# Parameter loads spread over three issuing queues in the opening of a two-layer hybrid SSD, Hyena and mLSTM kernel

## What is computed

```
mod  = silu(c) @ w_mod[i] + b_mod[i]          # six vectors of 1024, for latent and context
u    = modulated_norm(x, norm1_w[i], mod[0], mod[1]) @ w_in[i]
z, xbc, dt, hy_u, qk, v, o, g = split(u)      # three mixers: SSD, Hyena, mLSTM
hyena: uc = short_conv(hy_u, hy_conv_w, hy_conv_b)
       filt = (sin-MLP(feats) @ hy_pos_w3) * exp(-t * |hy_decay|), normalised, transformed
       z = gate * (long_conv(z, filt) + hy_skip * z), twice
x    = x + mod[2] * (concat(mixers) @ w_out[i])
x    = x + mod[5] * hier_moe(modulated_norm(x, norm2_w[i], mod[3], mod[4]))   # 32 experts, top-2
```

## Time and profile before

| | |
|---|---|
| median of 3 runs | 1327.77 us (1325.08 to 1328.37) |
| the profiled execution | 1324.55 us |
| its span in the profile | 1322.6 us |
| PE busy | 1170.5 us, 88% of the span |
| DVE busy | 605.8 us, 46% |
| ACT busy | 305.9 us, 23% |
| POOL busy | 133.2 us, 10% |
| DMA | 323.50 MB, mean 245 GB/s |

### The profile page before, as it was taken

The page is one execution under the profiler, slowest core; times in us unless marked ns, Lnnn a source line. Parts: engine busy times, 40 slices in busy tenths (PEclk is TensorE's granted clock), DMA queues, the critical chain, the costliest instruction groups (busy, mean ns, idle before and its releaser), DMA issues. The chain is left out here.

```text
span 1322.6 us, 19488 instructions
## 1 busy us (share of the span) xinstructions
PE 1170.5 (88%) x7596; PEld 769.2 (58%) x7596; DVE 605.8 (46%) x1233; ACT 305.9 (23%) x623; POOL 133.2 (10%) x144
## 2 busy tenths in 40 slices
PE   6799999999899979999877689998889899988882
PEld 3444547987678855555444466467768655545551
DVE  4424996037973641343111266973393533332223
ACT  4201112254552202131111233141442100000001
POOL 0000000000000012222221100000000112221220
PEclk9799999998999979999898899998999899998997
DMA  8653233236663579999999755441484879999982
GB/s 289 194 163 98 94 111 96 86 123 198 205 243 101 234 249 384 391 388 376 374 385 387 268 188 166 127 139 49 159 273 189 345 306 388 386 389 390 403 340 113
DMA packets 146965, 323.50 MB, mean 245 GB/s; under 512 B 28249, under 2 KB 111254, under 8 KB 121912
## 3 DMA queue, kind: packets, MB, share of 16 engines
q1 hardware_dynamic: 135384, 306.17, 63.8%
q0 software_dynamic: 11392, 15.79, 3.7%
q10 hardware_dynamic: 96, 0.26, 0.0%
HBM read 321.37 MB, written 22.28 MB: 260 GB/s over the span
## 5 line engine op out<-in xcount | busy, mean ns | idle before, releaser
L657 PE MATMUL bank<-hT,ring 128*128 128x512 f32 (+1 forms) x544 | 207.9, 540 | 1.8 <-DVE hT L1784 1.8
L657 PE MATMUL bank<-ring,hT 128*128 128x256 f32 (+1 forms) x928 | 180.3, 349 | 8.7 <-DVE chain L1794 3.9
L657 PEld LDWEIGHTS bank<-ring,hT 128*128 128x128 f32 x928 | 154.3, 194 | 27.8 <-issue 7.2
L657 PEld LDWEIGHTS bank<-hT,ring 128*128 128x128 f32 x544 | 104.5, 194 | 98.9 <-issue 91.9
L1788 DVE TENSOR_TENSOR ktok<-ktok,bank 64x256 f32<-64x256 f32 x65 | 27.5, 423 | 278.2 <-ACT ktok L1401 198.0
L657 PE MATMUL bank<-chain,qkT 128*64 128x256 f32 (+1 forms) x760 | 138.8, 380 | 6.1 <-DMA chain<-in_moe_w_up 2.7
L1401 ACT ACTIVATE ktok<-bank 64x256 f32<-64x256 f32 (+2 forms) x79 | 32.1, 406 | 346.9 <-PE bank L657 295.0
L657 PE MATMUL bank<-ring,qkT 128*64 128x256 f32 x512 | 92.7, 409 | 15.8 <-DMA ring<-in_moe_w_up 7.7
L1334 POOL DMA_INDIRECT pair_rows<-hyT,ysum x65 | 65.7, 1011 | 382.5 <-ACT hyT L1401 194.9
L657 PEld LDWEIGHTS bank<-chain,qkT 128*64 128x64 f32 (+1 forms) x760 | 82.6, 150 | 26.1 <-issue 4.8
L657 PEld LDWEIGHTS bank<-ring,qkT 128*64 128x64 f32 x512 | 56.3, 147 | 33.4 <-issue 15.1
(11 more groups left out here) (298 smaller groups left out, 1748.1 us busy)
## 6 DMA issues: line engine op xcount, KB each, us to landing
ring<-in_w_mod SPq DMA_DIRECT2D x40, 1024.0 KB
ring<-in_w_in SPq DMA_DIRECT2D x22, 1024.0 KB
chain<-in_moe_w_up SPq DMA_DIRECT2D x21, 1024.0 KB
chain<-in_moe_w_gate SPq DMA_DIRECT2D x19, 1024.0 KB
ring<-in_moe_w_down SPq DMA_DIRECT2D x18, 1024.0 KB
chain<-in_moe_w_down SPq DMA_DIRECT2D x17, 1024.0 KB
ring<-in_moe_w_gate SPq DMA_DIRECT2D x16, 1024.0 KB
ring<-in_moe_w_up SPq DMA_DIRECT2D x16, 1024.0 KB
```

The source lines that it names most:

```text
L657: return nc.tensor.matmul(o, a, b, start=s, stop=e, **k)
```

## The change

The small loads of the opening leave SP. ACT issues the six of the filter network, and POOL the rest, in the order: `tcol`, taps, the modulation biases of layer 0, norm weights, `dft`, the 9 rows of `prow`; then it waits until modulation part 7 is made and issues the gate columns and weights, the modulation biases of layer 1, the constants and the router's parameters (37 DMAs). `prow` has a semaphore of its own. SP issues the identity, the conditioning vectors, the tokens and then only large weights. The instructions of PE, ACT and DVE in the opening stand in another order, and the first `hy` block waits for `hT` column by column instead of for all of it, in both layers.

```
@@ small loads by a function that takes the engine, prow on its own semaphore
+        def fetch(eng, group, dst, src):
+            with nc.allow_non_contiguous_dma(reason="small parameters"):
+                eng.dma_start(dst, src).then_inc(tally.sems[group], tick(group, (group,), by=16))
...
+                fetch(eng, f"prow{l}_in", prow[r:r + n, :], src)
@@ SP, opening
-                    hidden_parameters(0)
-                    tap_parameters(0)
+                    fetch(sp, "cond_in", ident[:, :], A["const_ident"])
+                    fetch(sp, "cond_in", cond_v[:, :, 0], A["c"][0].rearrange("(p k) -> p k", k=KB))
+                    fetch(sp, "cond_in", cond_v[:, :, 1], A["c_ctx"].rearrange("(p k) -> p k", k=KB))
+                    fetch(sp, "x_in", x_v[:, 0:2, :], A["ctx"][0].rearrange("(t p) d -> p t d", p=P))
...
                     first_pair(0)
...
-                    fetch("dft_in", dft[:, :], A["const_dft"])
                     first_single(6)
-                    for layer in range(DEPTH):
-                        fetch("mod_bias_in", bmod_v[:, layer], A["b_mod"][layer].rearrange("(m p k) -> p m k", m=6, k=KB))
-                    norm_weights(0)
                     first_single(7)
@@ PE
                     filter_step(l, 2)
-                    modulation(l, 0)
-                    modulation(l, 1)
+                    pe.wait_ge(*due(("cond",)))
+                    for n in range(6):
+                        modulation(l, n)
+                    mod_vector(l, 0)
                     filter_step(l, 3)
...
-                    filter_step(l, 4)
-                    filter_step(l, 5)
                     modulation(l, 6)
                     modulation(l, 7)
                     mod_vector(l, 1)
...
-                    small_columns()
-                    pe.wait_ge(*due(("h1T", l, 0)))
-                    pe.wait_ge(*due(("h1T", l, 1)))
...
-                    pe.wait_ge(*due(("h1T", l, 1, "act")))
-                    pe.wait_ge(*due(("h1T", l, 1, "dve")))
...
+                            if (name, blk) == ("hy", 0):
+                                for s in range(1 if a0 else 0, 2):
+                                    pe.wait_ge(*due(("h1T", l, s, k)))
                             last = mm(b[:, a0:512], w[:, k, i * P:(i + 1) * P], hT_v[:, k, a0:512],
...
+                        if (l, name, blk) == (0, "hy", 0):
+                            small_columns()
...
                     channel_major("hy", 6, q, lambda blk: n0)
+                    if l == 0 and q == 0:
+                        pe.wait_ge(*due(("four",)))
+                        filter_step(l, 4)
+                        filter_step(l, 5)
@@ POOL, ahead of everything else
+            fetch(pool, "taps0_in", tcol[:, :], A["const_tcol"])
+            tap_parameters(pool, 0)
...
+            mod_biases(0)
+            norm_weights(pool, 0)
+            fetch(pool, "dft_in", dft[:, :], A["const_dft"])
+            parameters(pool, 0)
+            pool.wait_ge(*due(("made", ("mod", 0, 7))))
+            gate_parameters(pool, 0)
+            mod_biases(1)
+            for const, t in (("gsel", gsel), ("mask", ysum[:, 1024:1024 + 2 * P]), ("keep", keep), ("iom", iom), ("inv", inv)):
+                fetch(pool, "consts_in", t[:, :], A["const_" + const])
+            router_parameters(pool, 0)
@@ ACT: the six loads first, token squares between the two sines, and the sums of the taps behind rows 0 to 3
+            fetch(act, "hidden0_in", w1[0:POS, :], A["hy_pos_w1"][0])
...
@@ DVE: filter steps 4 and 5 behind the second hy block
+                    if l == 0 and blk == 2:
+                        filter_step(l, 4)
+                        filter_step(l, 5)
```

More of the change, by code:

```diff
@@ L177, in build @@
         cond_in = sem("cond_in")
-        mod_bias_in, nw_in = sem("mod_bias_in"), [sem(f"nw{l}_in") for l in range(DEPTH)]
+        mod_bias_in, nw_in = [sem(f"mod_bias{l}_in") for l in range(DEPTH)], [sem(f"nw{l}_in") for l in range(DEPTH)]
         dft_in = sem("dft_in")
@@ L182, in build @@
         consts_in, x_in, norm_in, out_written = sem("consts_in"), sem("x_in"), sem("norm_in"), sem("out_written")
+        prow_in = [sem(f"prow{l}_in") for l in range(DEPTH)]
         params_in = [sem(f"params{l}_in") for l in range(DEPTH)]
@@ L380, in build, with norm_weights, parameters @@
         held = {}
+        def fetch(eng, group, dst, src):
+            with nc.allow_non_contiguous_dma(reason="small parameters"):
+                eng.dma_start(dst, src).then_inc(tally.sems[group], tick(group, (group,), by=16))
+        def norm_weights(eng, l):
+            fetch(eng, f"nw{l}_in", nw_v[:, 0, :], A["norm1_w"][l].rearrange("(p k) -> p k", k=KB))
+            fetch(eng, f"nw{l}_in", nw_v[:, 1, :], A["norm2_w"][l].rearrange("(p k) -> p k", k=KB))
+        def parameters(eng, l):
+            if l:
+                eng.wait_ge(*due(("ab", l - 1, 1)))
+                norm_weights(eng, l)
+            r = 0
+            for name, n in (("ssd_conv_w", 15), ("ssd_conv_b", 5), ("hy_conv_w", 18), ("hy_conv_b", 6),
+                            ("ml_conv_w", 18), ("ml_conv_b", 6), ("ssd_norm_w", 3), ("ml_norm_w", 3),
+                            ("hy_skip", 4)):
+                src = A[name][l]
+                src = src.rearrange("w (b c) -> (w b) c", c=P) if len(src.shape) == 2 else \
+                    src.rearrange("(b c) -> b c", c=P)
+                fetch(eng, f"prow{l}_in", prow[r:r + n, :], src)
+                r += n
@@ new lines, in gate_parameters @@
+        def gate_parameters(eng, l):
+            g = f"params{l}_in"
+            if l == 0:
+                eng.wait_ge(*due(("gcolp zero",)))
+                eng.wait_ge(*due(("wgr zero",)))
+            for d in range(2):
+                for copy in range(3):
+                    s0, m0 = 32 * d + 8 * copy, 64 + 32 * d + 8 * copy
+                    fetch(eng, g, gcolp[s0:s0 + HEADS, 0:1], A["ssd_dt_bias"][l, d].unsqueeze(1))
+                    fetch(eng, g, gcolp[m0:m0 + HEADS, 0:1], A["ml_gate_b"][l, d, 1].unsqueeze(1))
+                    fetch(eng, g, gcolp[m0:m0 + HEADS, 1:2], A["ml_gate_b"][l, d, 0].unsqueeze(1))
+                    fetch(eng, g, gcolp[s0:s0 + HEADS, 2:3], A["ssd_a_log"][l, d].unsqueeze(1))
+            win = A["w_in"][l].rearrange("(p k) n -> p k n", k=KB)
+            fetch(eng, g, wgr_v[:, :, 0:12], win[:, :, COL_DT:COL_DT + 12])
+            fetch(eng, g, wgr_v[:, :, 12:36], win[:, :, COL_G:COL_G + 24])
+            fetch(eng, g, ssdd[:, :], A["ssd_d"][l].partition_broadcast(P))
@@ new lines, in hidden_parameters, with tap_parameters @@
+        def hidden_parameters(eng, l):
+            h = f"hidden{l}_in"
+            fetch(eng, h, w1[0:POS, :], A["hy_pos_w1"][l])
+            fetch(eng, h, w2[0:FH, :], A["hy_pos_w2"][l])
+            for c, name in enumerate(("hy_pos_b1", "hy_pos_b2", "hy_freq")):
+                fetch(eng, h, hcol[0:FH, c:c + 1], A[name][l].unsqueeze(1))
+        def tap_parameters(eng, l):
+            g = f"taps{l}_in"
+            fetch(eng, g, w3[0:FH, :], A["hy_pos_w3"][l])
+            fetch(eng, g, decays,
+                  A["hy_decay"][l].rearrange("e o c -> (e o c)").partition_broadcast(P))
@@ L954, in _ @@
                 if l:
[L955 removed]
+                    pe.wait_ge(*due(("h1T", l, 0, KB - 1)))
                 gate_sums()
@@ L1436, in _ @@
                 if l == 0:
-                    for n in range(3):
-                        filter_step(l, n)
-                    mod_rows(l, 0)
-                    mod_rows(l, 1)
-                    filter_step(l, 3)
+                    filter_step(l, 0)
                 else:
@@ L1914, in _ @@
                     step(V.memset(vaug[:, :], 1.0))
-                    for n in (1, 2, 3):
-                        filter_step(l, n)
+                    filter_step(l, 1)
+                    inverse(l, 0, NT)
+                    filter_step(l, 2)
                 def normed_input(t):
```

143 lines of the change are left out of this document (43 added, 100 removed).

## The result

The changed kernel takes **1314.69 us**, median of five runs (1313.79 to 1321.6), beside 1328.37 us for the kernel before (five runs, 1325.08 to 1330.06): a ratio of 0.9915, 95% interval 0.9893 to 0.9937. Its profiled execution took 1313.79 us with a span of 1312.0, against 1324.55 and 1322.6. Forecast were 1317.4 for the median and 1314.1 for the profiled execution. The changed kernel was timed twice more beside the experiments: 1318.25 against 1325.67, and 1316.61 against 1327.61.

A forecast was written before the change was run, and what follows sets the result against it. PE's opening waits for late loads and its low clock were taken to bound the kernel; 8.1 + 6.4 + 2.4 - 4.5 - 2.0 = 10.4 us, so 1327.77 - 10.4 = 1317.4 us, range 1311.5 to 1323.5.

The forecast's parts named there:

- Term A: Opening: part 7's product ends at 38.6 instead of 46.67 us; gain 8.1 us, bounds 6 and 9.7.
- So PE is what ends last: Opening, part 7: PE's own work ends at 38.6 us, against 37 by the load alone.
- The clock will be low at the start of it: Opening, PE's work behind the third 2 MB piece: low clock after the wait, 2.1 us added.
- take 29.8 us at 389 GB/s: Opening loads up to part 7: 11.6 MB at one rate, 29.8 us; part 7 lands at 35.9.
- Term B: Opening, from part 7 to the projection: 6.3 us instead of 12.7; gain 6.4, bounds 5.4 and 6.4.
- Term C: Projection's first piece in the opening: full clock, 14.00 instead of 16.65 us; gain 2.4, or 0 if clock low.
- Term D: Filter steps 4 and 5 move between the first and second `hy` piece: loss 4.5 us, bounds 3.5 and 6.
- Term E: Layer 1, context transposes: PE idles 5.6 us, work behind starts at half speed; loss 2.0 us, bounds 0 and 3.3.
- The first rival: Layer 1 costs nothing as the clock holds; opening gives 12.4 us or somewhat more: 1313 to 1315; chance 0.22.
- POOL's list: POOL's 37 DMAs after part 7: 0.85 us each, landed at 76, hidden by two `hy` pieces, priced at nothing.
- The second rival: POOL's list ends too late for `gate_sums`; decides at 1.37 us a DMA; gather's price lands at 145, time 1367; chance 0.08.
- The third rival: Opening's large stream starts no earlier, only the 36 to 40 us hole closes: sum 5, 1322 to 1323 us; chance 0.15.

The follow-up runs named there:

- the repeats: Changed kernel, no edit, timed twice more against the kernel before: 1318.25 us (ratio 0.9936) and 1316.61 us (0.9914).
- the late list: Changed kernel, but POOL's 37 loads wait for the fourth `hy` block instead of modulation part 7: 1328.18 us, 1.0008 of the kernel before.
- all columns in layer 0: Changed kernel, but the first `hy` block of layer 0 waits for the last column of `hT`: 1315.04 us in a single run.

## Why the prediction was right, point by point

**Term A** (8.1 forecast, 7.50 measured: 46.67 to 39.17; 6.97 and 7.20 in the repeats). The mechanism was right: early start of the flow and no hole. "So PE is what ends last" and "The clock will be low at the start of it" are right in both repeats: the third piece is used 1.5 us later than the forecast 30.7, parts 4 and 5 run at the low clock, and part 7's product follows PE's own work without a wait. In the first profile both are wrong. There the third piece came at 30.96 (the row names DVE as releaser, whose `big` ended 0.02 us before; with the filter steps moved back it ended at 31.64 and PE still started at 30.97, so it was the load), PEclk was 1.00, PE was ready for part 7 at 36.2, and the load ended last, at 38.10 instead of 35.9. The step "take 29.8 us at 389 GB/s" gave one rate to all bytes; the last 2.1 MB come in 1 KB rows at 348, which makes 0.6 of the 2.2 us. Some 0.6 more are the slower flow at the start (191, 375 and 311 GB/s in the three stretches from 4 to 10 us, 0.2 MB less than I had counted until then), and the rest is open. So PE's clock and the load are two ways to almost the same end, 39.17 to 39.70 where 38.6 was forecast. That it was hit within 1.1 us is in part luck: the load that decided came 1.5 us late in the repeats (third piece) and 2.2 us late in the first profile (part 7), while PE's work behind the third piece, low clock included, was priced 0.5 us too long in the repeats and 1.7 in the first.

**Term B** (6.4, measured 5.65: 39.17 to 46.23; 6.17 and 6.16 in the repeats). The missing 0.8 us of the first profile are the clock: I took the vector at full speed, but behind the 1.94 us idle the clock fell and it took 1.94 us. In the repeats it takes 1.14 and 1.13, and the term is right to 0.3 us. Together A and B give 13.1 to 13.4 us in all three, where 14.5 were forecast. The by-column start is right: without it some 3 us are lost.

**Term C** (2.4, measured 2.64). From the projection to its end with the modulation part 14.94 us instead of 17.58. Right.

**Term D** (-4.5, measured -4.43: 61.17 to 65.60). The price was right, but the reason that it was a pure loss was not: the cover under which the steps had run is gone with the wait for part 7, and against leaving them in their place the move gains 2.7 us. My sum, which counts against the kernel before, is not touched by that.

**Term E** (-2.0, measured -2.57, and 1.1 to 2.6 in three traces). Idle 5.46 us where 5.6 was forecast, and PEclk 0.50 behind it. Two experiments, one of which fills the idle stretch and one of which shortens it to 1.96 us, take the loss away. The first rival, that layer 1 costs nothing, falls with them.

**POOL's list.** Hidden, as forecast; 0.56 us a DMA, where 0.85 was taken and 1.37 would have decided. Loads of 1024 pieces take 0.89 to 0.92 us, those of 768 pieces 0.84 to 0.88 and those of a few pieces 0.50: some 0.4 ns a piece, not the 15 ns of the gather. The second rival's far bound had no ground (and its sum is 149, not 145: 76 and 73 us more); its mechanism has, as the late list shows. The estimate from the Trainium skill, SBUF — State Buffer, section Who interferes with whom, of some 115 us for the list did not come true either (and what would have waited is `gate_sums`, not the projection): the loads from 42.94 to 48.88 keep their 0.50 us beside DVE's 6.15 us of work on `hT`. Issued at once, the last three of the list ran beside DVE's scaling of the tokens (28.32 to 31.91) and took 0.98, 0.62 and 0.80 us instead of 0.89, 0.56 and 0.55, and DVE 3.59 instead of 3.12; that is all the lengthening there is to see. No run shows whether DVE was in the mode that the page speaks of.

**The third rival** (the stream starts no earlier) falls on the row at 6 to 8 us, 375 GB/s, against 221 at 8 to 10 before.

**The sum**: 7.50 + 5.65 + 2.64 - 4.43 is 11.36 (12.4 forecast), less 2.57 is 8.8 (10.4 forecast). The ends of the terms add to gains of 2.1 and 15.0, not 3 and 14.5 as stated; both hold what was measured. The other 1.8 us of the 10.6 in the spans lie in stretches that scatter by more. So the marks in the trace gave 1.6 us less than forecast, and the time itself, 1314.69, is 2.7 us below the forecast: that the first median lies on the better side is scatter and not merit. The other two medians of the changed kernel, 1318.25 and 1316.61, stand on either side of the forecast within 1 us.

## What to carry to other kernels

Small loads ahead of large ones cost the stream the time it takes to issue them, and the engines' orders are to be changed together with the queues: each alone gave 5.4 and 2.4 us here, both 11.4. When an edit makes an engine arrive early at a chain that it cannot hurry, look at the clock behind the new idle stretch; a few products without use cost nothing there, while keeping the old wait helped in one kernel and not in another. Read a mechanism from more than one profile of the same kernel: here the first profile and the repeats reached the same mark by different waits. Hold small loads that are needed late back until the large ones of the start have landed, then check how far from their deadline they end.

## What the hardware showed that I had not expected

- The length of a row in memory sets the rate of a load: 348 GB/s in 1 KB rows, 387 in 2 KB rows, up to 416 in rows of 8 KB, with the DMA share higher at the lower rate.
- Some 1.1 MB of small loads issued by POOL beside the stream kept 2.03 MB of large weights from arriving by 38 us, and their third piece was used 6.0 to 7.3 us late.
- A direct load on POOL costs 0.50 us, and 0.90 with 1024 pieces.
- The length of an idle stretch alone does not say whether the clock falls: it held across 2.52 us (before parts 4 and 5) and 2.59 us (all columns in layer 0), and fell behind 1.94 us before part 7. Ahead of these three PE had worked for 17.6, 8.2 and 5.2 us with no gap over 0.7 us; before the change it fell behind 2.52 us that followed 7.5 us of such work. It also fell behind 3.70, 3.97, 4.14 and 5.46 us in the places named above. What decides was not separated.
- The stretch from the second `hy` piece to the pairs of layer 1, with code that is the same, took 673.9 to 681.9 us over the profiles (that of the late list, whose wait lies in it, left out). No gain below 3 us can be read from whole times here; from marks in the trace it can, where these repeat.
